# Four-mixer decoder step: GpSimd computes the low halves of six w_in blocks, and products wait for high and low halves apart

## The chip, the core and the metric

The kernel runs on one core of one Trainium2 chip. The metric is the device time of one execution in microseconds, as the median of several runs. Engines are named as the profile names them: PE is TensorE (its weight loads are PEld), DVE is VectorE, ACT is ScalarE, POOL is GpSimd, and SP is SyncE, which here only issues loads of weights.

## What is computed

One inference step of a decoder trunk of two layers, for a prompt of 256 tokens and 32 sample tokens (T = 288 columns). Each layer is a SwiGLU feed-forward block (FFN), four recurrent mixers that share one input and one output projection, and a second FFN, each between two RMS norms. Cut to what matters:

```python
def swiglu(h, wg, wu, wd):
    return (jax.nn.silu(h @ wg) * (h @ wu)) @ wd

for l in range(DEPTH):                       # DEPTH = 2
    hdn = rmsnorm(x, ns[0])
    x = x + 0.5 * rmsnorm(swiglu(hdn, w_gate[0], w_up[0], w_down[0]), ns[1])
    hdn = rmsnorm(x, ns[2])
    mix, st_new = token_mixers(hdn, pos, p, st, chunk)   # hdn @ w_in, four mixers, @ w_out
    x = x + rmsnorm(mix, ns[3])
    hdn = rmsnorm(x, ns[4])
    x = x + 0.5 * rmsnorm(swiglu(hdn, w_gate[1], w_up[1], w_down[1]), ns[5])
```

All matrices are float32: D_MODEL is 1024, the FFN is 2816 wide, and the 15 blocks of w_in that matter here are 256 columns each.

## The kernel before

The weights pass through SBUF in blocks of 1024 rows by 256 columns, one block for each *position*. A layer has 87 positions: 34 for the first FFN, 15 for w_in (POS_IN and on, called here block 0 to block 14), 4 for w_out (POS_OUT and on) and 34 for the second FFN. SP loads a block into one of four slots of `ring`. ACT copies it, rounded to the fast float32r format, into one of two slots of `whigh` (`upper`, line 945; it counts `weights_high` up). DVE then subtracts the two and writes the remainder in place into `ring` (`lower_weights`, whose subtraction is line 1212; it counts `weights_split` up). These are the high and the low half of the block.

The activations are split in the same way, high half in `hdn` (or `big`), low half in `yR` (or `lowR`, `bigR`). PE's function `product` (its matmuls are line 468) multiplies 128 columns of a block with the activations in three groups of eight matmuls: high weights by high activations, low weights by high activations, high weights by low activations. A block gives two products, t = 0 and t = 1, so 48 matmuls of 128x128 by 128x288.

Every engine runs its own instruction list in order, and the lists meet only at semaphores. PE's `hold` is a wait followed by an increment of a semaphore of its own. Ahead of the first product of a block stands `slot_ready`, which is a hold for `weights_split`: the first matmul of a block waits until DVE has finished the low half. The first product after a norm (`ready` is given) also waits for each piece of the activations.

In the in-projection (w_in), product i of 30 belongs to block i // 2. Before it PE holds for `proj_read` of product i - 3 (ACT has emptied the PSUM bank). ACT's list per product is: wait for the product; if i is odd, `upper` of block (i + 3) / 2; read the product out of PSUM; then some gate work. DVE's list has the fifteen low halves among the convolutions (lines 1318 and 1320), the rotation of retention's q and k (lines 1360 to 1365), and the gates. After product 17 PE multiplies for the rotation, and after product 21 it needs DVE's decays.

At the w_out products PE holds for `last_read` (DVE's copy into `lastT`, line 1447), then `slot_ready`, then `y_done`. In DVE's list the first low half of w_out stands right behind that copy.

POOL issues the loads and stores of the recurrent states. In the in-projection it waits for DVE's `decays_ready` with the load of retention's state behind that wait, and then for the end of the projection.

Of the kernel before, what the change touches and what calls it, by code (L numbers as in the profile page):

```python
# [20 lines left out]
F32 = mybir.dt.float32  # L21
F32R = mybir.dt.float32r
ALU = mybir.AluOpType
# [55 lines left out]
assert POSITIONS % RING == 0  # L79
PER_SLOT = POSITIONS // RING  # L80
H_CREDIT = 2
Y_CREDIT = 4
# [92 lines left out]
def trunk_kernel(nc, I, O):  # L175
    ctx = ExitStack()
    with ctx:
# [288 lines left out]
        def _(pe):  # L466
# [12 lines left out]
            def slot_ready(l, pos, j=0):  # L479

                hold(sem("weights_split"), l * N_POS + pos + 1 + j * 4)

            hdnR = hdn[:, :, :].bitcast(F32R)

            def product(out, pos, t, rows, high, low_, start=True, stop=True, ready=None):

                wl, wh = ringR[:, pos % RING], whighR[:, pos % 2]
                cols = [slice(k * 256 + t * P, k * 256 + t * P + P) for k in range(rows)]
                for k in range(rows):
                    if ready is not None:  # L490
                        hold(sem("hdn_high"), ready[0] + k + 1)
                    mm(out, wh[:, cols[k]], high[:, k, :], start and k == 0, False)
                for k in range(rows):
                    mm(out, wl[:, cols[k]], high[:, k, :], False, False)
                for k in range(rows):
                    if ready is not None and k % 4 == 0:
                        hold(sem("hdn_low"), ready[1] + k // 4 + 1)
                    g = mm(out, wh[:, cols[k]], low_[:, k, :], False, stop and k == rows - 1)
                return g
# [17 lines left out]
            def ffn(l, f):  # L517
# [4 lines left out]
                def pair(pos, tile0, j):  # L522

                    for n, done in enumerate(("gate_done", "up_done")):
                        slot_ready(l, pos + n, j)
                        for t in range(2):

                            hold(sem("h_done" if n else "silu_done"), tile0 + t + 1)
                            product(ps[:, 2 * t + n, 0:T], pos + n, t, KT, hdnR, yR,
                                    ready=ready.pop() if ready else None)\  # L530
                                .then_inc(sem(done), 1)
# [9 lines left out]
                for mp in range(4):  # L541
                    for part, nk in enumerate(DOWN):
                        slot_ready(l, pos + 3 * mp + part)
                        ks = slice(8 * part, 8 * part + nk)
                        for t in range(2):
                            m = 2 * mp + t
                            if part == 0:
                                hold(sem("y_done"), l * 24 + post * 8 + m + 1)
                            d = product(ps[:, m % 4, 0:T], pos + 3 * mp + part, t, nk, bigR[:, ks], lowR[:, ks],
                                        part == 0, part == 2)  # L550
                            if part == 2:
                                d.then_inc(sem("post_product_done"), 1)
# [14 lines left out]
            def mixers(l):  # L567
# [61 lines left out]
                for i in range(NPT):  # L629
                    if i >= 4:  # L630
                        hold(sem("proj_read"), l * NPT + i - 3)
                    if i % 2 == 0:
                        slot_ready(l, POS_IN + i // 2)
                    product(ps[:, i % 4, 0:T], POS_IN + i // 2, i % 2, KT, hdnR, yR,
                            ready=None if i else (l * 24 + 8, l * 6 + 2)).then_inc(sem("proj_done"), 1)
                    if i == 1:
# [252 lines left out]
            with pe.Fori(0, DEPTH) as l:  # L889
# [7 lines left out]
                for i in range(4):  # L897
                    slot_ready(l, POS_OUT + i)
                    for t in range(2):
                        m = 2 * i + t  # L900
                        hold(sem("y_done"), l * 24 + 8 + m + 1)
                        product(ps[:, m % 4, 0:T], POS_OUT + i, t, KT, hdnR, bigR)\
                            .then_inc(sem("post_product_done"), 1)
# [266 lines left out]
        def _(dve):  # L1170
# [127 lines left out]
            def mixers(l):  # L1298
# [4 lines left out]
                def weights(n):  # L1303
                    lower_weights(l, POS_IN + n)

# [408 lines left out]
        def _(pool):  # L1714
# [32 lines left out]
            with pool.Fori(0, DEPTH) as l:  # L1747
# [24 lines left out]

                hold(sem("decays_ready"), l1)
                load_states("ret")

# [107 lines left out]
```

## Time and profile before

| what | value |
|---|---|
| device time, median of 3 runs | 1806.53 us (1803.3 to 1808.39) |
| span of the profiled execution, first to last instruction | 1796.3 us |
| PE busy with matmuls | 1592.9 us (89%) |
| DVE busy | 903.6 us (50%) |
| ACT busy | 556.7 us (31%) |
| POOL busy | 164.9 us (9%) |
| mean granted clock of PE | 0.871 |

The page gives for the profiled execution its span only, and no device time of its own; the median of the runs is 10.2 us above that span, which is what lies around the first and the last instruction. A share is of the span. PE's busy time says how long matmuls were in flight, and the rest of the span is where PE stood still.

### The profile page before, as it was taken

What the parts mean: (1) busy time and instruction counts of PE and PEld (TensorE: products, weight loads), DVE (VectorE), ACT (ScalarE), POOL (GpSimd) and SP (SyncE); (2) the same over time, 40 slices, a digit from 0 to 9 for tenths busy, and PEclk for the clock granted to TensorE, in tenths of its full rate; (3) what the DMA queues carried; (4) which work ended last, traced back from release to release, by engine and by line L of the source; (5) the groups of instructions that cost most, each with busy time, mean ns of one, the idle gap of its engine ahead of it and who ended that gap; (6) DMA issues with size and microseconds to landing.
All of it is one profiled execution on the core that took longest, in us unless ns stands there. A gap on an engine that the chain in (4) does not pass through costs nothing.

```text
span 1796.3 us, 28795 instructions
## 1 busy us (share of the span) xinstructions
PE 1592.9 (89%) x10846; PEld 1492.3 (83%) x10846; DVE 903.6 (50%) x1415; ACT 556.7 (31%) x752; POOL 164.9 (9%) x249
## 2 busy tenths in 40 slices
PE   4999989988787789999889999899788888899995
PEld 3999979977775679999879999799687757799994
DVE  4455455645454555553455544566363544655433
ACT  3333344440011143333353333454200111533331
POOL 6000000100133320000000000001002413000000
PEclk9999999988755589999989999899695556899997
DMA  8455443430011144554334545254101102255440
GB/s 194 149 166 164 159 136 116 148 101 1 3 30 33 12 115 139 164 164 139 117 121 163 164 152 176 71 165 129 48 1 26 26 14 64 95 163 163 142 163 27
DMA packets 184921, 194.17 MB, mean 108 GB/s; under 512 B 7284, under 2 KB 181700, under 8 KB 184688
## 3 DMA queue, kind: packets, MB, share of 16 engines
q1 hardware_dynamic: 176864, 178.27, 30.7%
q0 software_dynamic: 7376, 10.91, 3.5%
q10 hardware_dynamic: 576, 3.59, 0.5%
q8 instruction: 66, 1.08, 0.3%
q14 instruction: 39, 0.32, 0.1%
HBM read 186.55 MB, written 6.19 MB: 107 GB/s over the span
## 4 chain that ended last, share of the span: by engine, by line
PE 84%; DVE 7%; issue 5%; ACT 2%; DMA 1%; DVEq 0%; ACTq 0%; SPq 0%; POOL 0%
PE ps L468 82%; PE ps L471 2%; DVE y L1253 1%; DVE ring_r L1212 1%; DMA ring<-in_ffn_w_up 1%; DMA big<-in_x_sample 1%; DVE y L1670 0%; DVE arena L1483 0%; DVE x L1254 0%; ACT lnr L967 0%; DVE big L1590 0%; DVE big L1709 0%; ACT rrow L968 0%; DVE y L1227 0%; DVE Sbd L1552 0%
## 5 line engine op out<-in xcount | busy, mean ns | idle before, releaser
L1212 DVE TENSOR_TENSOR ring_r<-ring,whigh_r 128x2048 fp32r<-128x2048 f32 (+1 forms) x174 | 389.9, 2242 | 466.4 <-ACT whigh_r L945 466.1
L945 ACT ACTIVATE whigh_r<-ring 128x2048 fp32r<-128x2048 f32 (+1 forms) x174 | 326.2, 1875 | 481.6 <-PE ps L468 471.8
L468 PE MATMUL ps<-hdn,whigh_r 128*128 128x288 f32 x2016 | 328.4, 305 | 24.7 <-ACT hdn L955 15.0
L468 PEld LDWEIGHTS ps<-hdn,whigh_r 128*128 128x128 f32 x2016 | 292.3, 192 | 37.1 <-issue 31.8
L468 PE MATMUL ps<-hdn,ring_r 128*128 128x288 f32 x2016 | 315.9, 300 | 0.0
L468 PE MATMUL ps<-y_r,whigh_r 128*128 128x288 f32 x1888 | 293.4, 299 | 0.0
L468 PEld LDWEIGHTS ps<-hdn,ring_r 128*128 128x128 f32 x2016 | 288.1, 193 | 0.0
L468 PEld LDWEIGHTS ps<-y_r,whigh_r 128*128 128x128 f32 x1888 | 268.8, 191 | 0.0
L468 PE MATMUL ps<-big_r,whigh_r 128*128 128x288 f32 x832 | 130.4, 298 | 7.5 <-DVE arena_r L1212 7.5
L468 PEld LDWEIGHTS ps<-big_r,whigh_r 128*128 128x128 f32 x832 | 117.4, 190 | 8.5 <-issue 8.3
L468 PE MATMUL ps<-big_r,ring_r 128*128 128x288 f32 x704 | 110.9, 299 | 0.0
L468 PE MATMUL ps<-arena_r,whigh_r 128*128 128x288 f32 x704 | 109.8, 297 | 0.0
L468 PEld LDWEIGHTS ps<-big_r,ring_r 128*128 128x128 f32 x704 | 100.3, 191 | 0.0
L468 PEld LDWEIGHTS ps<-arena_r,whigh_r 128*128 128x128 f32 x704 | 100.1, 191 | 0.0
L994 ACT ACTIVATE sg<-ps 128x288 f32<-128x288 f32 x88 | 36.2, 411 | 182.7 <-PE ps L468 182.7
L1764 POOL DMA_DIRECT2D Sx<-in_state_ret x16 | 9.8, 627 | 897.9 <-DVE G L1373 897.5
L1135 ACT ACTIVATE arena<-onfin 128x768 f32<-128x768 f32 x6 | 5.1, 845 | 253.7 <-DVE onfin L1615 212.9
L468 PE MATMUL ps<-y,whigh 128*128 128x128 f32 x448 | 75.5, 289 | 6.1 <-DVE y L1670 4.6
L468 PE MATMUL ps<-y,cst 128*128 128x288 f32 x96 | 45.0, 636 | 31.5 <-ACT y L977 31.3
L468 PEld LDWEIGHTS ps<-y,whigh 128*128 128x128 f32 x448 | 63.7, 202 | 8.0 <-issue 7.8
L468 PEld LDWEIGHTS ps<-y,cst 128*128 128x128 f32 x96 | 25.8, 292 | 49.5 <-ACT y L977 43.1
L471 PE MATMUL ps<-cst,big 128*128 128x128 f32 (+2 forms) x114 | 29.1, 414 | 30.6 <-DMA big<-in_x_sample 13.9
(328 smaller groups left out, 1624.4 us busy)
## 6 DMA issues: line engine op xcount, KB each, us to landing
ring<-in_ffn_w_gate SPq DMA_DIRECT2D x44, 1024.0 KB, 5.2
ring<-in_ffn_w_up SPq DMA_DIRECT2D x44, 1024.0 KB, 5.2
ring<-in_ffn_w_down SPq DMA_DIRECT2D x32, 1024.0 KB, 5.1
ring<-in_w_in SPq DMA_DIRECT2D x30, 1024.0 KB, 5.0
ring<-in_ffn_w_down SPq DMA_DIRECT2D x16, 768.0 KB, 4.4
ring<-in_w_out SPq DMA_DIRECT2D x8, 1024.0 KB, 5.4
cst<-in_const ACTq DMA_DIRECT2D x1, 2301.0 KB, 8.3
big<-in_x_prompt ACTq DMA_DIRECT2D x1, 1024.0 KB, 11.4
```

Source lines behind the costliest of these rows:

```text
L468: return pe.matmul(out, lhsT, rhs, start=start, stop=stop, **k)
L471: return pe.transpose(out, in_, ident[0:in_.shape[0], 0:in_.shape[0]])
L945: A(whighR[:, pos % 2, 0:rows * 256], ring[:, s, 0:rows * 256], ACT.Copy)\
L994: A(sg[:, t, :], ps[:, 2 * t, 0:T], ACT.Silu).then_inc(sem("silu_done"), 1)
L1135: A(osq, on, ACT.Square).then_inc(sem("out_sq"), 1)
L1212: return TT(out, in_, high, ALU.subtract)
L1253: link(l, STT(y[:, k, :], y[:, k, :], g_[:, i, k:k + 1], rrow[:, :], ALU.mult, ALU.mult))
L1764: dma(dst, src).then_inc(sem("states_loaded_" + m), 16)
```

## The change

Three things change.

1. `slot_ready` waits for `weights_high` (ACT's half alone). A new `low_ready` is a second hold, ahead of the first group that reads the low half.
2. In every product but the first after a norm, the order of the groups becomes high by high, high weights by low activations, low weights by high activations, so that the low half of the weights is used last. `low_ready` stands there in the product t = 0 only.
3. The low halves of blocks 3, 5, 7, 9, 11 and 13 of w_in (`POOL_POS`) leave DVE's list and go to POOL's, with a semaphore of their own. POOL issues the load of retention's state, which it did behind its wait for `decays_ready`, between blocks 11 and 13.

```diff
+POOL_POS = tuple(POS_IN + n for n in range(3, N_IN, 2))
...
             def slot_ready(l, pos, j=0):
-                hold(sem("weights_split"), l * N_POS + pos + 1 + j * 4)
+                hold(sem("weights_high"), l * N_POS + pos + 1 + j * 4)
+
+            def low_ready(l, pos, j=0):
+                if pos in POOL_POS:
+                    hold(sem("weights_split_pool"), l * len(POOL_POS) + POOL_POS.index(pos) + 1)
+                else:
+                    before = sum(p < pos for p in POOL_POS)
+                    hold(sem("weights_split"), l * (N_POS - len(POOL_POS)) + pos + 1 - before + j * 4)
...
                     mm(out, wh[:, cols[k]], high[:, k, :], start and k == 0, False)
-                for k in range(rows):
-                    mm(out, wl[:, cols[k]], high[:, k, :], False, False)
+                if ready is not None:
+                    low_ready(l, pos, j)
+                    for k in range(rows):
+                        mm(out, wl[:, cols[k]], high[:, k, :], False, False)
                 for k in range(rows):
                     if ready is not None and k % 4 == 0:
                         hold(sem("hdn_low"), ready[1] + k // 4 + 1)
-                    g = mm(out, wh[:, cols[k]], low_[:, k, :], False, stop and k == rows - 1)
+                    g = mm(out, wh[:, cols[k]], low_[:, k, :], False, stop and ready is not None and k == rows - 1)
+                if ready is None:
+                    if t == 0:
+                        low_ready(l, pos, j)
+                    for k in range(rows):
+                        g = mm(out, wl[:, cols[k]], high[:, k, :], False, stop and k == rows - 1)
                 return g
...
                 def weights(n):
-                    lower_weights(l, POS_IN + n)
+                    if POS_IN + n not in POOL_POS:
+                        lower_weights(l, POS_IN + n)
...
                 load_states("gdn")
-                hold(sem("decays_ready"), l1)
-                load_states("ret")
+                for pos in POOL_POS:
+                    if pos == POS_IN + 13:
+                        hold(sem("decays_ready"), l1)
+                        load_states("ret")
+                    pool.wait_ge(sem("weights_high"), l * N_POS + pos + 1)
+                    pool.tensor_tensor(ringR[:, pos % RING], ring[:, pos % RING],
+                                       whighR[:, pos % 2].bitcast(F32), ALU.subtract)\
+                        .then_inc(sem("weights_split_pool"), 1)
```

PE's list at the start of the w_out products, first before the change and then after it. `last` and `cst` feed the transposes that DVE copies into `lastT`; `hdn` is the high half of the activations here and `big_r` the low half, and the REGISTER_ALU rows prepare or count a hold.

```order
L471 MATMUL ps<-cst,last 27x128 x9
L476 REGISTER_ALU [waits last_read]
L468 MATMUL ps<-hdn,whigh_r 128x288 [waits weights_split,y_done]
L468 MATMUL ps<-hdn,whigh_r 128x288 x7
L468 MATMUL ps<-hdn,ring_r 128x288 x8
L468 MATMUL ps<-big_r,whigh_r 128x288 x8
```

```order
L472 MATMUL ps<-cst,last 27x128 x9
L477 REGISTER_ALU [waits last_read]
L469 MATMUL ps<-hdn,whigh_r 128x288 [waits weights_high,y_done]
L469 MATMUL ps<-hdn,whigh_r 128x288 x7
L469 MATMUL ps<-big_r,whigh_r 128x288 x8
L477 REGISTER_ALU
L469 MATMUL ps<-hdn,ring_r 128x288 [waits weights_split]
L469 MATMUL ps<-hdn,ring_r 128x288 x7
```

The wait for DVE's half has moved from the first matmul to the seventeenth, and one register instruction has come in ahead of it. The holds ahead of the first matmul are as many as before.

PE's list over product t = 0 of block 3 of w_in, before and then after, up to the start of t = 1; `ring_r` is the low half of the weights and `y_r` the low half of the activations.

```order
L476 REGISTER_ALU [waits proj_read]
L468 MATMUL ps<-hdn,whigh_r 128x288 [waits weights_split]
L468 MATMUL ps<-hdn,whigh_r 128x288 x7
L468 MATMUL ps<-hdn,ring_r 128x288 x8
L468 MATMUL ps<-y_r,whigh_r 128x288 x8
L476 REGISTER_ALU
L468 MATMUL ps<-hdn,whigh_r 128x288 [waits proj_read]
```

```order
L477 REGISTER_ALU [waits proj_read]
L469 MATMUL ps<-hdn,whigh_r 128x288 [waits weights_high]
L469 MATMUL ps<-hdn,whigh_r 128x288 x7
L469 MATMUL ps<-y_r,whigh_r 128x288 x8
L477 REGISTER_ALU
L469 MATMUL ps<-hdn,ring_r 128x288 [waits weights_split_pool]
L469 MATMUL ps<-hdn,ring_r 128x288 x7
L477 REGISTER_ALU
L469 MATMUL ps<-hdn,whigh_r 128x288 [waits proj_read]
```

The third group now waits for POOL; before, the first waited for DVE.

POOL's list over the in-projection, before and then after. `Sx<-in_state_ret` is the load of retention's state, and `MEMSET whigh` waits for the end of the projection.

```order
L1718 REGISTER_ALU
L1764 DMA Sx<-in_state_ret 64x4x64 [waits decays_ready]
L1764 DMA Sx<-in_state_ret 64x4x64 x7
L1718 REGISTER_ALU
L1777 MEMSET whigh 128x1152 [waits proj_done]
```

```order
L1795 TENSOR_TENSOR ring_r<-ring,whigh_r 128x2048 [waits weights_high]
L1735 REGISTER_ALU
L1781 DMA Sx<-in_state_ret 64x4x64 [waits decays_ready]
L1781 DMA Sx<-in_state_ret 64x4x64 x7
L1794 REGISTER_ALU
L1795 TENSOR_TENSOR ring_r<-ring,whigh_r 128x2048 [waits weights_high]
L1735 REGISTER_ALU
L1800 MEMSET whigh 128x1152 [waits proj_done]
```

The first row of the second list is the last of five such subtractions that stand ahead of the load of the state; the sixth stands behind it.

## Rows read from the trace of the kernel before

**Rows 1.** The page: busy time of each engine, and the low halves' group (count, busy, mean ns).
```profile
PE 1592.9 (89%) x10846; PEld 1492.3 (83%) x10846; DVE 903.6 (50%) x1415; ACT 556.7 (31%) x752; POOL 164.9 (9%) x249
...
L1212 DVE TENSOR_TENSOR ring_r<-ring,whigh_r 128x2048 fp32r<-128x2048 f32 (+1 forms) x174 | 389.9, 2242 | 466.4 <-ACT whigh_r L945 466.1
```

**Rows 2.** Waits of PE over the span: us in total, times, longest.
```profile
PE ps L468 <- DVE ring_r L1212: 9.2, 4, 4.2
```

**Rows 3.** Timeline, layer 0, w_in block 10: start, length, engine, line, operation, idle before.
```profile
346.42 2.29 DVE L1212 TENSOR_TENSOR ring_r<-ring,whigh_r 128x2048 fp32r<-128x2048 f32 x1
...
347.13 1.23 PE L468 MATMUL ps<-y_r,whigh_r 128*128 128x288 f32 x8
348.47 1.92 ACT L945 ACTIVATE whigh_r<-ring 128x2048 fp32r<-128x2048 f32 x1 [2.86 <-PE ps L468]
...
348.85 1.30 PE L468 MATMUL ps<-hdn,whigh_r 128*128 128x288 f32 x8 [0.50 <-DVE ring_r L1212]
```

**Rows 4.** Timeline, layer 1, the same place.
```profile
1223.78 1.23 PE L468 MATMUL ps<-y_r,whigh_r 128*128 128x288 f32 x8
...
1225.34 0.90 PE L468 MATMUL ps<-hdn,whigh_r 128*128 128x288 f32 x5 [0.33 <-DVE ring_r L1212]
```

**Rows 5.** Timeline, layer 0, start of the w_out products.
```profile
623.18 1.61 DVE L1447 COPY lastT<-ps 27x512 f32<-27x512 f32 x3 [1.25 <-PE ps L471]
...
624.72 4.47 DVE L1212 TENSOR_TENSOR ring_r<-ring,whigh_r 128x2048 fp32r<-128x2048 f32 x2
...
627.26 1.94 PEld L468 LDWEIGHTS ps<-hdn,whigh_r 128*128 128x128 f32 x8 [4.63 <-issue]
```

**Rows 6.** Timeline, layer 1, the same place.
```profile
1502.76 1.61 DVE L1447 COPY lastT<-ps 27x512 f32<-27x512 f32 x3 [1.26 <-PE ps L471]
...
1506.83 1.94 PEld L468 LDWEIGHTS ps<-hdn,whigh_r 128*128 128x128 f32 x8 [4.63 <-issue]
```

**Rows 7.** Timeline, layer 0, start of the down products of the first FFN.
```profile
183.71 0.46 DVE L1212 TENSOR_TENSOR arena_r<-arena,big_r 128x288 fp32r<-128x288 f32 x1
184.67 1.09 PEld L468 LDWEIGHTS ps<-big_r,whigh_r 128*128 128x128 f32 x8 [2.07 <-issue]
```

**Rows 8.** Timeline of PE, in-projection of layer 0.
```profile
297.16 1.23 PE L468 MATMUL ps<-hdn,whigh_r 128*128 128x288 f32 x8
...
308.87 1.23 PE L468 MATMUL ps<-y_r,whigh_r 128*128 128x288 f32 x8
309.94 1.23 PE L468 MATMUL ps<-hdn,whigh_r 128*128 128x288 f32 x8
...
322.71 1.23 PE L468 MATMUL ps<-hdn,whigh_r 128*128 128x288 f32 x8
```

**Rows 9.** Timeline of ACT there: high halves of blocks 3, 5 and 7.
```profile
290.62 1.92 ACT L945 ACTIVATE whigh_r<-ring 128x2048 fp32r<-128x2048 f32 x1 [2.80 <-PE ps L468]
...
303.88 1.92 ACT L945 ACTIVATE whigh_r<-ring 128x2048 fp32r<-128x2048 f32 x1 [1.85 <-PE ps L468]
...
316.60 1.92 ACT L945 ACTIVATE whigh_r<-ring 128x2048 fp32r<-128x2048 f32 x1 [2.79 <-PE ps L468]
```

**Rows 10.** Groups by line and form: count, busy us, mean ns.
```profile
L1785 POOL TENSOR_TENSOR whigh<-arena,cst 32x512 f32<-32x512 f32 x28 | 29.3, 1079 | 162.7 <-DVE y L1670 154.8 <-ACT arena L1113 8.0
...
L1777 POOL MEMSET whigh<- 128x1152 f32 x2 | 2.1, 1057 | 66.6 <-PE ps L468 66.6
```

**Rows 11.** Timeline of DVE, in-projection of layer 0.
```profile
303.77 0.19 DVE L1333 TENSOR_TENSOR U<-ps,gbias 128x40 f32<-128x40 f32 x1
...
308.05 0.41 DVE L1318 TENSOR_SCALAR big<-arena,taps,cbias 128x256 f32<-128x256 f32 x1
308.49 1.53 DVE L1320 SCALAR_TENSOR_TENSOR big<-arena,taps,big 128x256 f32<-128x256 f32 x3
```

**Rows 12.** Windows of PE, w_out products: stretch, its length, busy (count), granted clock, DMA.
```profile
631.00:632.00 1.00, 1.00 (x7) 0.70 0.38 31
...
1512.00:1513.00 1.00, 1.00 (x8) 0.88 0.49 115
```

More of the change, by code:

```diff
@@ L479, in slot_ready, with product @@
             def slot_ready(l, pos, j=0):
-                hold(sem("weights_split"), l * N_POS + pos + 1 + j * 4)
+                hold(sem("weights_high"), l * N_POS + pos + 1 + j * 4)
[5 more added lines that the diff above has]
+                    hold(sem("weights_split"), l * (N_POS - len(POOL_POS)) + pos + 1 - before + j * 4)
             hdnR = hdn[:, :, :].bitcast(F32R)
-            def product(out, pos, t, rows, high, low_, start=True, stop=True, ready=None):
+            def product(out, pos, t, rows, high, low_, start=True, stop=True, ready=None, l=None, j=0):
                 wl, wh = ringR[:, pos % RING], whighR[:, pos % 2]
@@ L529, in pair @@
                             product(ps[:, 2 * t + n, 0:T], pos + n, t, KT, hdnR, yR,
-                                    ready=ready.pop() if ready else None)\
+                                    ready=ready.pop() if ready else None, l=l, j=j)\
                                 .then_inc(sem(done), 1)
@@ L549, in ffn @@
                             d = product(ps[:, m % 4, 0:T], pos + 3 * mp + part, t, nk, bigR[:, ks], lowR[:, ks],
-                                        part == 0, part == 2)
+                                        part == 0, part == 2, l=l)
                             if part == 2:
@@ L634, in mixers @@
                     product(ps[:, i % 4, 0:T], POS_IN + i // 2, i % 2, KT, hdnR, yR,
-                            ready=None if i else (l * 24 + 8, l * 6 + 2)).then_inc(sem("proj_done"), 1)
+                            ready=None if i else (l * 24 + 8, l * 6 + 2), l=l).then_inc(sem("proj_done"), 1)
                     if i == 1:
@@ L901, in _ @@
                         hold(sem("y_done"), l * 24 + 8 + m + 1)
-                        product(ps[:, m % 4, 0:T], POS_OUT + i, t, KT, hdnR, bigR)\
+                        product(ps[:, m % 4, 0:T], POS_OUT + i, t, KT, hdnR, bigR, l=l)\
                             .then_inc(sem("post_product_done"), 1)
```

## The prediction

> **What bounds the kernel now.** I read the page first. PE is busy for 1592.9 of 1796.3 us, DVE for 903.6 and POOL for 164.9 [rows 1]. So PE sets the time, and a change helps only where PE stands still or where its matmuls become fewer or quicker. Here no matmul goes away: the three groups of a product are only put in another order. What is left is PE's standing still.
>
> The next view is therefore PE's own waits. Of all the time in which PE was idle, the low halves of the weights (`ring_r`, DVE's line 1212) account for 9.2 us in 4 waits, the longest 4.2 us [rows 2]. That is the whole stock from which the change can draw; DVE writes 174 such halves [rows 1], and for 170 of them PE never waited. The timelines show where the four lie: two at block 10 of w_in, one in each layer [rows 3, 4], and two at the start of the w_out products [rows 5, 6].
>
> The timeline of PE inside the in-projection shows the rest of it at full pace. Product 6 starts at 297.16, product 10 at 309.94 and product 14 at 322.71 [rows 8]: four products of 24 matmuls take 12.78 us, 0.133 us a matmul, 1.065 us for a group of eight. Relieving DVE there gives nothing by itself, because nobody waited for it.
>
> **What the split of the wait gives at w_out.** DVE's copy into `lastT` ends at 623.18 + 1.61 = 624.79, and with it `last_read` is there. PE's first weight load comes at 627.26, because `slot_ready` waits for the low half that DVE starts only behind that copy [rows 5]. After the change `slot_ready` needs ACT's half alone, which is long done, and PE waits for `last_read` only. How long PE then takes is not nil: the hold for `last_read` is followed by two more, `slot_ready` and `y_done`. The same chain of three holds stands at the start of the down products, where DVE ended at 183.71 + 0.46 = 184.17 and PE's first load came at 184.67 [rows 7], so 0.50 us. PE would load at 625.29 and gain 627.26 - 625.29 = 1.97 us. In layer 1 it is 1502.76 + 1.61 + 0.50 = 1504.87 against 1506.83 [rows 6], 1.96 us.
>
> Does the low half become the next wait? DVE starts two of them at 624.72 for 4.47 us together [rows 5], so the first is done near 627.0. PE reads it after sixteen matmuls; its loads for the first eight took 1.94 us at the clock granted there [rows 5], so it gets there at about 625.3 + 3.9 = 629.2. There are 2.2 us to spare.
>
> **What it gives at block 10.** The last group of product 19 starts at 347.13, and the next product could start 1.065 later, at 348.20. It started at 348.85, because DVE was late with the low half after the rotation: 346.42 + 2.29 = 348.71 [rows 3]. Gain 0.65 us. In layer 1 it is 1223.78 + 1.065 = 1224.85 against 1225.34 [rows 4], 0.49 us. The low half is then needed after two groups, at 350.33, and is there at 348.71. PE next needs things from ACT and DVE that are not moved later by the change, and it was not waiting in the products behind this one, so the gain stays.
>
> **Sum.** 1.97 + 1.96 + 0.65 + 0.49 = 5.07 us, out of the 9.2 us of the view of waits; what remains of them is the wait for the copy into `lastT` and the latency of the holds.
>
> **What the change adds on PE.** One hold for each of 87 positions in 2 layers, 174 in all, inside a product that is running. The nearest row for its price when the semaphore is already up is the border between two products. Between 308.87 and 309.94 PE passed two holds (`proj_read` and `slot_ready`) and the groups still stood 1.07 us apart [rows 8], against 1.065 for a group without any. So a hold that lies under running matmuls costs 0 to 0.01 us, 0 to 1.7 us in all. I take 0, since four products with six holds between them show no excess.
>
> **What it adds on POOL.** Twelve subtractions of 128x2048. The trace of before has none of that size on POOL. From above the nearest row is the one tensor_tensor that POOL runs, 32x512 in 1079 ns, 2.11 ns an element, so 4.32 us for 2048; from below it is the memset, 1057 ns for 1152 elements, which would make 1.88 us [rows 10]. A subtraction reads two inputs as the tensor_tensor does, so I take 4.32; as the far end I keep twice that, 8.63, for an operation over four times the partitions and beside a busy DVE.
>
> Its cover is the time from ACT's half to PE's third group. ACT's halves of blocks 3, 5 and 7 end at 292.54, 305.80 and 318.52 [rows 9]; PE's third groups would start 2.13 us into products 6, 10 and 14, at 299.29, 312.07 and 324.84 [rows 8]. The cover is 6.75, 6.27 and 6.32 us, so at 4.32 us POOL is 1.95 to 2.43 us early. Blocks 9, 11 and 13 have more, because PE has other work in between. Cost 0 at 4.32 us; without cover each microsecond beyond it would count in three blocks of each layer.
>
> Here the Trainium skill has a figure for exactly this operation: "GPSIMD Engine Reference", section 3.1, gives 4497 ns for a float32 tensor_tensor of 2048 elements on GpSimd, near the 4.32 us that I scaled from the row. By the page's figure the spare time would be 1.8 us and the sum the same.
>
> **POOL beside DVE.** In layer 0 DVE has finished the gates' additions soon after 304 (the first stands at 303.77) and would then run convolution 3, which takes 0.41 + 1.53 us, up to 306.3, since block 5's low half no longer stands ahead of it [rows 11]. POOL starts at 305.80. Should the one wait for the other, POOL is 0.5 us late at most and ends at 310.6, before 312.07; and a convolution that is 4.3 us late has room, as the row of before ends it at 308.49 + 1.53 = 310.02 anyway. The Trainium skill speaks against the change at this place: "SBUF — State Buffer", section "Who interferes with whom", says that a VectorE instruction with two SBUF inputs and a GpSimd instruction that reads SBUF exclude each other for a whole instruction. By that rule the overlap costs 0.5 us of POOL's spare time and nothing on PE; no row of before shows the two side by side.
>
> POOL's load of retention's state moves behind its fifth subtraction, by about 4 us; It is an issue of transfers only, and the state is read only in the second mixer.
>
> **The time.** All terms are differences inside the one profiled span of 1796.3 us. Against the median of the runs, 10.2 us above it, they stay the same: 1806.5 - 5.1 = 1801.4 us. The runs themselves lie between 1803.3 and 1808.4, and some 0.3%, 5.4 us, is what a measurement of this kernel can tell from no change. The forecast lies just inside it.
>
> **Rivals.**
> - *Clock.* After the wait at w_out PE runs at the lower of its two clocks (1.2 of 2.4 GHz). The rows of windows put the rise at 631.60 (0.70 is 0.6 us at half) and 1512.24 (0.88) [rows 12], which is 4.3 and 5.4 us after the first load. With 2 us less idle time the rise could come sooner. At the most, with full clock from the start, that gives half of 9.7 us, 4.9 us more; I price it at half of that, 2.4 us: 1799.0. Against it: PE was busy and at half clock long before this wait too. Chance 0.20.
> - *The holds swallow part.* If the start at w_out takes longer than 0.50 us behind `last_read`, or the 174 holds cost their 0.01 us, 1.5 to 3 us are left: 1804. Chance 0.10.
> - *POOL is the bound (slower).* At 8.63 us a subtraction PE waits 1.88, 2.36 and 2.31 us in blocks 3, 5 and 7, 6.6 us a layer, 13.1 us in all: 1814.6. It decides from 7.3 us on, where 3 x 7.3 less the cover of 19.3 us is half of 5.07; from 8.2 us on it is slower by over 0.3%. Nothing in the rows points above 4.5 us except that none has 128 partitions. Chance 0.07.
> - *A hold inside a product stops PE (slower).* Laid open, three holds took 0.50 us [rows 7], so one may cost up to 0.17 us, and 174 of them 29 us: 1831. It decides from 0.03 us each. The spacing of 1.07 us speaks against it. Chance 0.04.
> - *The forecast*, 3 to 7 us gained. Chance 0.59.
>
> **The numbers.** The forecast's own range is 1799.5 to 1803.5; about four tenths of its chance lie beyond 5.4 us. Faster by over 0.3%: 0.59 x 0.4 + 0.17 of the clock's 0.20 = 0.40. Slower: 0.07 + 0.04, of which 0.01 is too small to tell, 0.10. The rest, 0.50, is no change. The range that should hold 8 in 10 reaches from the clock's case less what the median of a few runs may be off, 1797, to just above the case of the swallowed gain with a small cost of POOL, 1808.
>
> **What would show it.** In the profile after, PE's waits for `ring_r` from DVE should be gone or below 1 us, with a wait of some 2.2 us for DVE's line 1447 in their place; the first w_out load should stand 0.5 us behind the copy. POOL should have twelve rows of about 4.3 us with no PE wait behind them, DVE's count of low halves should fall from 174 to 162, and the groups of matmuls should stay 1.065 us apart across the new hold. The prediction is wrong if PE waits for POOL, if the groups are further apart at the third group of t = 0, or if the clock rises at another time than 4 to 5 us after the start.

## The result, and the profile after

| | median of runs (range) | span of the profiled execution | ratio to before (95%) |
|---|---|---|---|
| before | 1804.26 us (1801.54 to 1808.39, 5 runs) | 1796.3 us | |
| changed | 1794.88 us (1788.03 to 1797.39, 5 runs) | 1788.7 us | 0.9939 [0.9916, 0.9961] |

The kernel became 0.6% faster, 9.4 us by the medians, nearly twice the 5.07 us of the forecast; 1794.88 lies below the forecast range of 1797 to 1808. The device time of the changed kernel's profiled execution is 1790.26 us, so 1.6 us lie around its span, not the 10.2 us that the prediction put there (1.5 to 1.8 us in nearly all of the runs below, 3.0 at the most). All medians and ratios of this document are of fast runs, which leaves out one run, of POOL only with six more matmuls (3654.42 us).

The page's line of busy times, against [rows 1]:

```profile
PE 1587.4 (89%) x10846; PEld 1488.9 (83%) x10846; DVE 886.0 (50%) x1403; ACT 556.4 (31%) x752; POOL 220.3 (12%) x261
```

PE has as many matmuls as before and is busy for 5.5 us less. This matters more than it looks. The change takes no matmul away, so the waits that went cannot lower PE's busy time. The same matmuls took less time.

The waits of PE (line waited for: us in total, times, longest), against [rows 2]:

```profile
PE ps L469 <- ACT y L993: 32.3, 14, 8.7
...
PE ps L469 <- DVE lastT L1464: 4.5, 2, 2.2
```

The row for `ring_r` is gone, and there is none for POOL. In its place stand two waits of 2.2 us for the copy into `lastT`.

The timeline at block 10, layer 0 (start, us; idle time and releaser in brackets), against [rows 3]:

```profile
349.01 1.23 PE L469 MATMUL ps<-y_r,whigh_r 128*128 128x288 f32 x8
349.35 2.29 DVE L1228 TENSOR_TENSOR ring_r<-ring,whigh_r 128x2048 fp32r<-128x2048 f32 x1
350.07 1.23 PE L469 MATMUL ps<-hdn,ring_r 128*128 128x288 f32 x8
351.14 1.23 PE L469 MATMUL ps<-hdn,whigh_r 128*128 128x288 f32 x8
```

DVE's subtraction for block 10 runs from 349.35 to 351.64. Block 10's first group starts at 351.14 all the same, 1.07 us behind the group before it. In the kernel before this start had to wait, 1.72 us behind the group before it. In layer 1 the two distances are 1.56 us before and 1.06 us now.

The start of the w_out products in layer 0 and then in layer 1, against [rows 5, 6]:

```profile
626.17 1.61 DVE L1464 COPY lastT<-ps 27x512 f32<-27x512 f32 x3 [1.26 <-PE ps L472]
627.71 4.47 DVE L1228 TENSOR_TENSOR ring_r<-ring,whigh_r 128x2048 fp32r<-128x2048 f32 x2
628.29 1.94 PEld L469 LDWEIGHTS ps<-hdn,whigh_r 128*128 128x128 f32 x8 [2.67 <-issue]
628.32 2.26 PE L469 MATMUL ps<-hdn,whigh_r 128*128 128x288 f32 x8 [2.24 <-DVE lastT L1464]
630.38 2.12 PE L469 MATMUL ps<-big_r,whigh_r 128*128 128x288 f32 x8
...
1496.53 1.61 DVE L1464 COPY lastT<-ps 27x512 f32<-27x512 f32 x3 [1.25 <-PE ps L472]
1498.64 1.94 PEld L469 LDWEIGHTS ps<-hdn,whigh_r 128*128 128x128 f32 x8 [2.67 <-issue]
1498.67 2.26 PE L469 MATMUL ps<-hdn,whigh_r 128*128 128x288 f32 x8 [2.24 <-DVE lastT L1464]
```

The copy ends at 627.78 and the first weight load stands at 628.29, 0.51 us behind it, where before it stood 2.47 us behind it: 1.96 us. In layer 1 it is 0.50 us instead of 2.46, again 1.96.

POOL's group, and two of its twelve subtractions in the timeline:

```profile
L1795 POOL TENSOR_TENSOR ring_r<-ring,whigh_r 128x2048 fp32r<-128x2048 f32 x12 | 55.5, 4627 | 868.4 <-ACT whigh_r L961 868.4
```

```profile
308.84 4.77 POOL L1795 TENSOR_TENSOR ring_r<-ring,whigh_r 128x2048 fp32r<-128x2048 f32 x1 [8.69 <-ACT whigh_r L961]
...
353.41 4.60 POOL L1795 TENSOR_TENSOR ring_r<-ring,whigh_r 128x2048 fp32r<-128x2048 f32 x1 [14.41 <-ACT whigh_r L961]
```

And PE around block 5's third group, the one that reads what POOL wrote from 308.84 to 313.61:

```profile
313.96 1.23 PE L469 MATMUL ps<-y_r,whigh_r 128*128 128x288 f32 x8
315.02 1.23 PE L469 MATMUL ps<-hdn,ring_r 128*128 128x288 f32 x8
```

The hold for POOL lies between these two rows; they are 1.06 us apart, and POOL was 1.41 us early.

### Where the time came from

I lined the two traces up matmul by matmul, by their ordinal number. Ahead of product 2 of w_in in layer 0 both programs run the same matmuls on PE, the changed one in its new order of groups, and no wait for a low half lies there. But executions differ there (PE reached product 2 at 283.9 us before and at 286.8 us after). So everything from here on counts from that product's first matmul to the start of the last matmul of the kernel. This length is 1502.74 us before and 1492.15 us after, 10.59 us less. The waits are 5.07 us of it. The other 5.5 us are spread over places in which no wait was taken away:

| place | before | after | difference |
|---|---|---|---|
| waits: block 10, 0.65 and 0.50; w_out, 1.96 and 1.96 | | | -5.07 |
| norm behind w_out, layer 0 | 14.93 | 12.98 | -1.95 |
| norm ahead of w_in, layer 1 | 15.79 | 13.84 | -1.95 |
| norm behind w_out, layer 1 | 12.98 | 14.64 | +1.66 |
| norms between the layers | 22.09 | 21.48 | -0.61 |
| w_out products, layers 0 and 1, start to end | 58.46 | 58.20 | -0.26 |
| mixers, layers 0 and 1, first matmul behind w_in to the last transpose of `last` | 460.53 | 458.91 | -1.62 |
| all else | | | -0.8 |

The windows show what these places have in common. The columns are the window, its length, PE's busy time with its matmuls, the granted clock as a share of full speed, and DMA share and GB/s. Before: all from product 2 on, the norm ahead of w_in in layer 1, and the norm behind w_out in layer 0.

```profile
283.85:1796.26 1512.41, 1341.31 (x9122) 0.85 0.32 99
1130.60:1146.40 15.80, 9.90 (x20) 0.68 0.21 67
656.28:671.21 14.93, 9.17 (x18) 0.66 0.22 71
```

After:

```profile
286.80:1788.66 1501.86, 1333.71 (x9121) 0.86 0.33 100
1129.35:1143.19 13.84, 7.36 (x20) 0.87 0.25 76
658.19:671.17 12.98, 7.03 (x19) 0.87 0.24 80
```

The norm in layer 1 has twenty matmuls in both rows, at a clock of 0.68 before and 0.87 after. The timeline of that norm shows which ones. Before:

```profile
1134.21 3.25 PE L468 MATMUL ps<-y,cst 128*128 128x288 f32 x6 [2.85 <-ACT y L977]
1138.19 5.17 PE L468 MATMUL ps<-y,cst 128*128 128x288 f32 x10 [0.73 <-ACT y L977]
```

After:

```profile
1133.35 3.15 PE L469 MATMUL ps<-y,cst 128*128 128x288 f32 x6 [2.84 <-ACT y L993]
1137.32 2.31 PE L469 MATMUL ps<-y,cst 128*128 128x288 f32 x8 [0.82 <-ACT y L993]
1139.80 0.75 PE L469 MATMUL ps<-y,cst 128*128 128x288 f32 x2 [0.17 <-ACT y L993]
```

Before, the last ten matmuls ran without a break at half clock (1.2 of 2.4 GHz), 5.17 us, and PE set the pace. After, ten took 3.23 us, with a wait for ACT between them. The clock rose there within the norm after and not before. Over the whole stretch from product 2 on, the granted clock of short windows adds up to 445.0 us at half clock before and 420.8 us after.

### The profile page after: what moved, and what is told of

Read it like the earlier page. It is cut to its first block, busy times and chain, and to the rows that moved or that the text cites. A ratio compares the mean times of both kernels' runs of the same rounds, so it can differ in the third digit from the quotient of the medians.

```text
span 1788.7 us, 29119 instructions
## 1 busy us (share of the span) xinstructions
PE 1587.4 (89%) x10846; PEld 1488.9 (83%) x10846; DVE 886.0 (50%) x1403; ACT 556.4 (31%) x752; POOL 220.3 (12%) x261
## 4 chain that ended last, share of the span: by engine, by line
PE 85%; DVE 7%; issue 4%; ACT 2%; DMA 1%; DVEq 0%; ACTq 0%; SPq 0%; POOL 0%
PE ps L469 82%; PE ps L472 2%; DVE y L1269 1%; DMA ring<-in_ffn_w_up 1%; DMA big<-in_x_sample 1%; DVE ring_r L1228 1%; DVE y L1687 0%; DVE arena L1500 0%; DVE x L1270 0%; ACT lnr L983 0%; DVE big L1607 0%; DVE big L1726 0%; ACT rrow L984 0%; DVE Sbd L1569 0%; DVE y L1243 0%
## 5 line engine op out<-in xcount | busy, mean ns | idle before, releaser
L1228 DVE TENSOR_TENSOR ring_r<-ring,whigh_r 128x2048 fp32r<-128x2048 f32 (+1 forms) x162 | 362.4, 2238 | 469.7 <-ACT whigh_r L961 469.2
L1795 POOL TENSOR_TENSOR ring_r<-ring,whigh_r 128x2048 fp32r<-128x2048 f32 x12 | 55.5, 4627 | 868.4 <-ACT whigh_r L961 868.4
L469 PE MATMUL ps<-y,cst 128*128 128x288 f32 x96 | 41.1, 588 | 32.6 <-ACT y L993 32.3
L472 PE MATMUL ps<-cst,big 128*128 128x128 f32 (+2 forms) x114 | 29.1, 415 | 30.6 <-DMA big<-in_x_sample 14.0
```

Source lines behind the costliest of these rows:

```text
L469: return pe.matmul(out, lhsT, rhs, start=start, stop=stop, **k)
L472: return pe.transpose(out, in_, ident[0:in_.shape[0], 0:in_.shape[0]])
L1228: return TT(out, in_, high, ALU.subtract)
L1795: pool.tensor_tensor(ringR[:, pos % RING], ring[:, pos % RING], whighR[:, pos % 2].bitcast(F32), ALU.subtract)\
```

## The experiments

The theories, by the letters that the expectations use:

- **Theory A:** the gain is the four waits alone, and the rest of the 9.4 us is the scatter of the medians. Its rival D is a second, regular gain; its rival C is a gain of the new order by itself.
- **Theory F (the waits, and where the clock falls):** the regular gain is the four waits. The further 5 us come from where the stretches at half clock fall in the work, and any small shift deals a new pattern.
- **Theory B (POOL's relief is worth something by itself):** DVE and the buffers come free sooner, and some of the 5 us is a lasting gain of the six blocks on POOL.
- **Theory G:** the clock plays no part, and the gain should stay the same however the program is shifted.

All numbers are gathered in one table behind the experiments. "From product 2" is the stretch defined above.

### One part at a time

*No POOL, against the changed kernel:* the wait split and the groups reordered, all low halves on DVE. The split wait in the old order of groups was not run.

```diff
-POOL_POS = tuple(POS_IN + n for n in range(3, N_IN, 2))
+POOL_POS = ()
...
-                for pos in POOL_POS:
...
+                hold(sem("decays_ready"), l1)
+                load_states("ret")
```

> The change without its third part: DVE computes all low halves, PE waits for high and low halves apart and uses the low half last. Theory A (the gain is PE's two waits, at block 10 and at the w_out products, and POOL is idle company): the whole gain is here, the same time as the changed kernel, 5 to 9 us below the kernel before. Rival B (DVE's relief by POOL matters): a clear part of the gain is missing, the time is 3 us or more above the changed kernel. In the profile by A no wait of PE for ring_r, and the two w_out starts 1.96 us earlier behind the copy into lastT.

*POOL only, against the changed kernel:* POOL keeps its six blocks, but `slot_ready` waits for the low half (DVE's or POOL's) ahead of the block, and the groups stand in the old order.

```diff
             def slot_ready(l, pos, j=0):
-                hold(sem("weights_high"), l * N_POS + pos + 1 + j * 4)
-
-            def low_ready(l, pos, j=0):
-
...
-                if ready is None:
-                    if t == 0:
-                        low_ready(l, pos, j)
-                    for k in range(rows):
-                        g = mm(out, wl[:, cols[k]], high[:, k, :], False, stop and k == rows - 1)
```

> The third part alone: POOL computes six low halves a layer, PE waits for the low half ahead of a block's first matmul, in the old order of the groups. Theory A: POOL is 4.6 us a block, ACT's half of blocks 3, 5 and 7 ends 4.62, 4.14 and 4.19 us ahead of PE's first matmul of the block, so PE waits 0 to 0.6 us in each of three blocks a layer, and the time is 0 to 3 us above the kernel before. Rival B: DVE's relief is worth something by itself, and the time is 2 us or more below the kernel before.

*Order only, against the kernel before:* the groups in the new order, the wait where it was.

```diff
+                if ready is None:
+                    for k in range(rows):
+                        g = mm(out, wl[:, cols[k]], high[:, k, :], False, stop and k == rows - 1)
```

> The order of the groups alone: high by high, high by low activations, low by high last; PE waits for the low half ahead of a block's first matmul as before, DVE computes all. Theory A: the order is worth nothing by itself, within 2 us of the kernel before, and the same four waits of PE for ring_r, 9.2 us. Rival C (the new order runs better on PE, in its clock or in its weight loads): 2 us or more below the kernel before, with PE's mean granted clock above 0.871 or groups closer than 1.065 us.

*The changed kernel once more*, without an edit.

> The changed kernel once more. Theory A (5.1 us of waits, the rest of the measured 9.4 us is the scatter of the medians): its median falls between 4 and 10 us below the kernel before, most likely nearer to 5 than the first measurement. Rival D (there is a second, regular gain of about 4 us): 9 us or more again.

Measured, in one series: no POOL 0.9957 [0.9944, 0.997], POOL only 0.9975 [0.996, 0.9991], order only 0.9986 [0.997, 1.0001], the changed kernel 0.9937 [0.9913, 0.9962]. From product 2 on they took 1498.90, 1496.56, 1502.76 and 1492.17 us.

Theory A, which took the excess for scatter, missed three of these four. No POOL came 3.2 us above the changed kernel of the series, where it wanted the same time. POOL only came 6.5 us below the kernel before, where it wanted 0 to 3 us above. The changed kernel came 11.3 us below again, where it wanted 4 to 10.

Three things follow. First, the order by itself does nothing: 1502.76 us against 1502.74, with the same 9.2 us of waits and a mean clock of 0.869; its timed runs, 2.2 us quicker, have an interval that reaches 1. Second, the changed kernel's two profiles (1492.15 and 1492.17) have the same length to 0.02 us, so the 5.5 us are not the accident of one execution alone. Their half-clock times are 420.8 and 424.2 us, so that number is good to some 3 us. Third, POOL by itself seems to bring 6.2 us, although all four waits for DVE are still there, and PE even waits for POOL, once for each of four blocks, as that kernel's waits and timeline show:

```profile
PE ps L469 <- DVE ring_r L1217: 9.4, 4, 4.2
...
PE ps L469 <- POOL ring_r L1784: 2.0, 4, 0.6
```

```profile
314.56 1.30 PE L469 MATMUL ps<-hdn,whigh_r 128*128 128x288 f32 x8 [0.55 <-POOL ring_r L1784]
```

With 2.2 us more of waiting, its stretch is 6.2 us shorter, so 8.4 us have to come from elsewhere. Its time at half clock is 414.4 us instead of 445.0. Here theory B and theory F say different things. By B these 6.2 us are a property of POOL's blocks and stay. By F they are the deal of this one program.

### The same programs, shifted

To deal again without changing a wait or a low half, the last matmul of the q/k norms, which PE runs behind product 27 of w_in, is repeated 2, 4 or 6 more times in each layer. The output is the same. The same edit goes into the kernel before, the changed kernel, no POOL and POOL only.

```diff
-                    for n in range(4):
+                    for n in (0, 1, 2, 3) + (3,) * 2:
```

The price of the added work, first in the kernel before and then with two more matmuls:

```profile
379.96 2.18 PE L468 MATMUL ps<-arena,cst 128*128 128x288 f32 x8
381.76 1.44 PE L468 MATMUL ps<-hdn,whigh_r 128*128 128x288 f32 x8
```

```profile
384.55 3.15 PE L468 MATMUL ps<-arena,cst 128*128 128x288 f32 x12
387.33 1.44 PE L468 MATMUL ps<-hdn,whigh_r 128*128 128x288 f32 x8
```

The way to the next product is 1.80 us and then 2.78 us, so 0.98 us a layer and 1.96 us in all. For four more and six more I take 3.92 and 5.88 us; the same way in layer 0 of those two profiles is 3.75 and 4.71 us, which makes 3.90 and 5.82. These are subtracted below.

The kernel before, shifted:

> The kernel before with two repeated matmuls (same operands, same output) behind the last of the four q and k norm matmuls of each layer: 0.45 us each on PE by the row of before, 0.9 us a layer, 1.8 us in all, so that everything behind them comes 0.9 us later. Theory F (the stretches in which the clock stands at its lower level fall differently when the work is shifted, and with them some us either way): the span less the added 1.8 us is up to 6 us away from the kernel before, either way, and the windows at half clock change behind the shifted place. Rival G (clock plays no part, the changed kernel has a regular gain beside the waits): 1.8 us more than the kernel before, to within 1 us.

> The kernel before with four repeated matmuls there, 1.8 us a layer, 3.6 us in all. Theory F: the span less 3.6 us is up to 6 us away from the kernel before, by another amount than with two. Rival G: 3.6 us more, to within 1 us.

> The kernel before with six repeated matmuls there, 2.7 us a layer, 5.4 us in all. Theory F: up to 6 us away from 5.4 us more. Rival G: 5.4 us more, to within 1 us.

The changed kernel, shifted:

> The changed kernel with two repeated matmuls there, 1.8 us in all. Theory F: its distance to the kernel before with the same two is not the 9 to 11 us measured without them; over the shifts of none, two, four and six matmuls the distance scatters by several us around 5.2 us, the two waits. Rival G: the distance is 9 to 11 us at every shift.

> The changed kernel with four repeated matmuls of the q and k norms in each layer, 3.6 us in all. Theory F: the distance to the kernel before with the same four is anywhere from 0 to 11 us, and the mean over the shifts is near 5.2 us. Rival G: 9 to 11 us.

> The changed kernel with six repeated matmuls there, 5.4 us in all. Theory F: the distance to the kernel before with the same six is anywhere from 0 to 11 us, and the mean over the shifts is near 5.2 us. Rival G: 9 to 11 us.

No POOL, shifted:

> The change without POOL's part, with two repeated q and k norm matmuls a layer (0.49 us each, as the runs before showed, 2.0 us in all). Open is whether the gain beyond the two waits is regular and due to POOL (rival B) or only where the stretches at half clock fall (theory F). From the in-projection of layer 0 to the end, without the added work, the kernel before took 1502.7, 1501.0, 1502.3 and 1504.2 us at the four shifts, mean 1502.6, the changed kernel 1492.2, 1490.2, 1495.5 and 1498.6, mean 1494.1. Theory F: this variant's mean over four shifts is 1494 to 1498, not to be told from the changed kernel. Rival B: 1497 or more, at every shift 3 us above the changed kernel.

> The same with four repeated matmuls a layer, 3.9 us in all; theory F: above or below the changed kernel by up to 5 us without order; rival B: about 3 us above it.

> The change without POOL's part with six repeated matmuls a layer, 5.9 us in all; theory F and rival B as for two and four.

POOL only, shifted:

> POOL's part alone with two repeated matmuls a layer. Without them it took 1496.6 us from the in-projection on, 6.2 us less than the kernel before, though PE waited 2.0 us for POOL. Theory F: that was where the half clock fell; at this shift the gain is another, and the mean over four shifts is 1502.6 + 2.0, with a scatter of 2 us. Rival B: 4 to 6 us below the kernel before at every shift.

> The same with four repeated matmuls a layer. Theory F: again another distance to the kernel before, near +2 us in the mean over the shifts. Rival B: 4 to 6 us below.

> POOL's part alone with six repeated matmuls a layer; theory F and rival B as for two and four.

All that was measured. "Net" is the time from product 2 on less the added work; "half clock" is the time in that stretch that PE's clock stood at 1.2 GHz, added up over short windows. Each ratio is to the kernel before as it ran in the same series; its medians there were 1802.72 to 1806.53 us. Lengths and half clock are of one profiled execution each.

| program | median us | ratio to before (95%) | from product 2 | net | half clock |
|---|---|---|---|---|---|
| before | 1804.26 | | 1502.74 | 1502.74 | 445.0 |
| before, +2 | 1803.07 | 0.9998 [0.9981, 1.0015] | 1502.91 | 1500.95 | 441.1 |
| before, +4 | 1806.16 | 1.0019 [0.9997, 1.004] | 1506.20 | 1502.28 | 448.5 |
| before, +6 | 1806.64 | 1.0024 [1.0007, 1.0041] | 1510.09 | 1504.21 | 445.1 |
| order only | 1802.44 | 0.9986 [0.997, 1.0001] | 1502.76 | 1502.76 | 441.6 |
| POOL only | 1798.19 | 0.9975 [0.996, 0.9991] | 1496.56 | 1496.56 | 414.4 |
| POOL only, +2 | 1802.73 | 0.9999 [0.9986, 1.0012] | 1505.58 | 1503.62 | 441.0 |
| POOL only, +4 | 1803.20 | 1.0002 [0.9983, 1.0021] | 1505.52 | 1501.60 | 434.1 |
| POOL only, +6 | 1812.12 | 1.0033 [1.0004, 1.0061] | 1511.52 | 1505.64 | 441.3 |
| no POOL | 1796.49 | 0.9957 [0.9944, 0.997] | 1498.90 | 1498.90 | 441.2 |
| no POOL, +2 | 1793.74 | 0.9952 [0.993, 0.9974] | 1499.37 | 1497.41 | 441.1 |
| no POOL, +4 | 1803.15 | 0.9999 [0.9981, 1.0017] | 1502.26 | 1498.34 | 444.5 |
| no POOL, +6 | 1801.62 | 0.9985 [0.9967, 1.0003] | 1499.48 | 1493.60 | 427.4 |
| changed | 1794.88 | 0.9939 [0.9916, 0.9961] | 1492.15 | 1492.15 | 420.8 |
| changed, again | 1793.33 | 0.9937 [0.9913, 0.9962] | 1492.17 | 1492.17 | 424.2 |
| changed, +2 | 1795.34 | 0.997 [0.9953, 0.9988] | 1492.18 | 1490.22 | 424.2 |
| changed, +4 | 1795.97 | 0.996 [0.9942, 0.9979] | 1499.41 | 1495.49 | 437.7 |
| changed, +6 | 1798.32 | 0.9981 [0.9962, 1.0] | 1504.52 | 1498.64 | 444.5 |

The distances of the net time to the equally shifted kernel before are, for +0, +2, +4 and +6:

| | +0 | +2 | +4 | +6 | mean |
|---|---|---|---|---|---|
| POOL only | -6.2 | +2.7 | -0.7 | +1.4 | -0.7 |
| no POOL | -3.8 | -3.5 | -3.9 | -10.6 | -5.5 |
| changed | -10.6 | -10.7 | -6.8 | -5.6 | -8.4 |

PE's waits for low halves are the same at every shift: 9.0 to 9.3 us in the kernel before, 9.3 or 9.4 for DVE and 2.0 or 2.1 for POOL in POOL only, none in the other two. So what moves in a row of this table is not a wait for a low half.

*POOL only* decides against theory B in the size that it had: 4 to 6 us at every shift. The distances are 6.2 us gained, then 2.7 lost, and the mean is 0.7 us gained. Theory F missed here too, the other way. With its 2.2 us of added waits POOL only should have had a mean net time of 1502.6 + 2.0 us, and it has 1501.9. *The changed kernel* has a gain of 10.6, 10.7, 6.8 and 5.6 us; theory G wanted 9 to 11 at every shift. *No POOL* has a mean of 5.5 us, close to the 5.1 us of the four waits, with one deal far off (-10.6, at the lowest half-clock time of its row).

The timed runs give similar means. Each ratio divided by that of the equally shifted kernel before, and averaged over the four shifts, gives 0.9952 for the changed kernel, 0.9963 for no POOL and 0.9992 for POOL only, about 8.6, 6.7 and 1.4 us. By the intervals of the ratios each of the three is good to some 2.3 us, an estimate that leaves out any scatter from shift to shift. The four ratios of POOL only so divided are 0.9975, 1.0001, 0.9983 and 1.0009; those of the changed kernel are 0.9939, 0.9972, 0.9941 and 0.9957. By these alone the gain of the changed kernel could be one and the same at all four shifts.

### What the shifts do not separate

The shift stands behind product 27 of w_in, so it can't change what the clock did ahead of product 2. Yet the profiles differ there. In ten of them the last two falls of the clock ahead of product 2 stand 24.3 and 14.1 us before its first matmul, to within 0.1 us; call them group 1. In six they stand some 27 and 13.5 us before it (group 2), and in two 25.5 and 11.8 us (group 3). The stretch from 28.0 to 24.5 us ahead of product 2 shows it, first in the kernel before and then in POOL only; the columns are those of the windows above, and the clock is 1.00 and 0.62:

```profile
255.85:259.35 3.50, 0.75 (x2) 1.00 0.82 273
```

```profile
259.50:263.00 3.50, 1.64 (x4) 0.62 0.51 176
```

The net times, sorted by group:

| | group 1 | group 2 | group 3 |
|---|---|---|---|
| before | 1502.74, 1502.28 (+4) | 1500.95 (+2), 1504.21 (+6) | |
| order only | 1502.76 | | |
| POOL only | 1503.62 (+2), 1501.60 (+4) | 1496.56 | 1505.64 (+6) |
| no POOL | 1498.90, 1498.34 (+4) | 1497.41 (+2), 1493.60 (+6) | |
| changed | 1492.15, 1492.17, 1490.22 (+2) | 1495.49 (+4) | 1498.64 (+6) |

Within group 1 a shift moves a program by 2.0 us at the most, and the gain of the changed kernel is 10 us or more with and without it. The two steps that spoke for theory F, POOL only from +0 to +2 and the changed kernel from +2 on, both go with a change of group. In group 2 the shift by itself moves the kernel before by 3.3 us and no POOL by 3.8. So the net time depends on what the execution brings along as well as on the program. That any small shift deals a new pattern is not shown, and the agreement of the changed kernel's two profiles to 0.02 us is that of two executions of one group.

The timed runs show the same from another side. Each has its span and its mean granted clock on record, and so its time at half clock, 2 x (1 - clock) x span. Among 121 runs of the unaltered kernel before that time goes from 452 to 503 us. Over 276 timed runs, each taken against the mean of its own program in its series, a run with 1 us more at half clock is 0.26 us longer (correlation 0.78). This speaks against the first half of theory G: the clock does play a part in a run's time. The averages over the four shifts are 478 us at half clock for the kernel before and 476 for no POOL, but 470 for POOL only and 468 for the changed kernel, with standard errors of 1.3 to 1.9.

So theory B is alive in a smaller size. Both programs with six blocks on POOL spend some 7 us less at half clock than their counterparts without them, which at 0.26 us each is worth 2 us, an estimate. In the traces POOL gives 2.9 us between no POOL and the changed kernel, and 0.7 + 2.2 = 2.9 us between the kernel before and POOL only, if its own waits are taken out; in the timed runs it is 1.9 and 3.6 us. Against that, the four distances between changed and no POOL in the traces are -6.8, -7.2, -2.9 and +5.0 us, with a standard error of 2.8 us. A lasting 2 to 4 us is likely and not shown, and why the clock should fall less is open.

## Why the prediction was wrong

**The wait at w_out: right.** Forecast 1.97 and 1.96 us, measured 1.96 and 1.96. The start behind the copy takes 0.51 and 0.50 us, as in the row from the down products. Both waits for `lastT` are 2.2 us, as announced.

**The wait at block 10: right.** Forecast 0.65 and 0.49, measured 0.65 and 0.50 us. The sum of 5.07 us came out as 5.07.

**The low half is not the next wait: right.** No row of PE waits for `ring_r`.

**The holds cost nothing: right.** Across the new hold the groups stand 1.06 to 1.07 us apart, and the three groups of a product take as long as before.

**POOL is covered: right, and larger than forecast.** Its subtraction took 4.63 us in the mean, between 4.32 us as scaled and 8.63 us as the far end. The longest was 4.77 us. The Trainium skill's 4497 ns ("GPSIMD Engine Reference", section 3.1) is nearer; all twelve here are above it, the shortest at 4577 ns by the rows grouped by tile. POOL's spare time was less than the 1.95 to 2.43 us of the forecast, 1.41 us at block 5 and 1.63 at block 7. And of blocks 9, 11 and 13, which were to have more, block 13 had only 1.75 us (7.88 and 3.21 at the other two).

**POOL beside DVE: right in kind, at another place.** The prediction looked at block 5 alone. There a convolution's three steps (307.61 to 309.13) were nearly over when POOL started at 308.84, and neither was held up by more than some tenths. At block 11 they had just begun. DVE's timeline has both, block 5 first:

```profile
307.61 1.52 DVE L1337 SCALAR_TENSOR_TENSOR big<-arena,taps,big 128x256 f32<-128x256 f32 x3
...
352.88 5.94 DVE L1337 SCALAR_TENSOR_TENSOR big<-arena,taps,big 128x256 f32<-128x256 f32 x3
```

The same three operations took 5.94 us instead of 1.52, and POOL's subtraction of 4.60 us (353.41 to 358.01) lies inside them. DVE stood for 4.4 us, nearly the whole of POOL's instruction. By the rule of the Trainium skill ("SBUF — State Buffer", section "Who interferes with whom") the two exclude each other for a whole instruction; the trace agrees. Nobody on PE waited for that convolution, so it cost nothing. The prediction should have gone through all six blocks, since a convolution with less room would have turned this into a wait.

**What failed: "All terms are differences inside the one profiled span ... they stay the same", and "so the gain stays".** These sentences treat everything behind a removed wait as a block that slides forward unaltered, and so put the change in the matmuls' own time at nothing. It was more than the waits: of the 10.59 us between the profiles 5.07 are the waits and 5.5 the rest, and PE's busy time fell by 5.5 us. The two profiles are of one group, so they entered product 2 alike. Here the norm behind w_out in layer 0 and the norm ahead of w_in in layer 1 each became 1.95 us shorter, the norm behind w_out in layer 1 became 1.66 us longer, and the balance with the mixers and the rest is 5.5 us of gain in this pair. That the clock does this is shown by the matmuls of the norms, by the 24 us less at half clock, and by the timed runs; why each single stretch falls where it does is not. Nor is it luck of one execution alone: over four shifts the gain is 8.6 us in the timed runs and 8.4 in the traces, 3.5 and 3.3 us above the waits.

**The rival "Clock" had the right engine and the wrong place.** It looked for the gain only at the start of w_out, where the rise was to come sooner, at 2.4 us. There the rise came 6.2 us after the first load in layer 0 (before 4.3) and 2.8 us in layer 1 (before 5.4): one later, one sooner, both outside the 4 to 5 us that the prediction had set as a sign, and almost nothing in the sum, -0.26 us for the products. Its upper bound of 4.9 us would have been the right size for the whole kernel, but on both sides of zero: over the shifts the three variants' distances lie between 5.5 us below and 3.4 us above their own means, and even the kernel before spreads over 3.3 us net.

**The baseline.** 1806.53 us was a median of three runs. Five runs have 1804.26, and later series 1802.7 to 1806.5. That makes 2.3 us of the miss of 6.5. With it goes the wrong reading that 10.2 us lie around the span. With some 1.6 us around it, the profiled execution of the kernel before took about 1798 us and was quicker than all five.

**The range.** It took in the costs of the change from both sides, but for what the change doesn't touch it had 2.4 us, and downwards only as far as one place. With 5 us of clock pattern in either direction around 1801.4 less the error of the median, it would have begun at about 1794.

## What to carry to other kernels

When PE sets the time, add up PE's waits for the thing that is to be made quicker: the part of that sum that the change can take away (here 5.1 of 9.2 us) was hit to 0.1 us. It is not the whole gain. On average over the shifts the changed kernel gained 8.6 us, and the rest went with less time at half clock. The waits went with waiting for the high half alone and using the low half last; relieving the engine that nobody waited for took away no wait, and its lasting worth, 2 to 4 us by these runs, is less than they can prove.

A gain or loss under 0.5% that is measured on one pair of profiles is part change and part clock pattern, and two profiles that agree do not show that all executions do. Measure several harmless shifts of both kernels, average their timed runs, compare the clock's record in them as well, and give a blind forecast a range that has this spread on both sides.

## What the runs showed of the hardware that was not expected

- Two profiles of the same program agree to 0.02 us over 1492 us of work, while two executions of programs that differ by 2 us of matmuls lay 7.1 us apart net (POOL only, +0 and +2). They had entered the work with another clock pattern, and the timed runs of the same two programs differ by far less: 1798.19 and 1802.73 us, 2.6 us net by their medians.
- Among the programs the half-clock time went from 414.4 to 448.5 us. Against the kernel before, the changed kernel had 24.2 us less of it and 5.5 us less time beyond the waits; POOL only had 30.6 us less and 8.4 us less time beyond the waits. That is about a quarter of a microsecond for each at half clock, an estimate from these two pairs, and the timed runs give 0.26: much of the work at half clock is where PE waits for others anyway, as in the norm with its wait for ACT.
- A subtraction of 128x2048 on POOL takes 4.58 to 4.77 us, and one that runs beside a chain of three short DVE operations lengthens that chain by 4.4 us.
